# Five more slots for expert weights in the mixers' memory, and a new order of the experts' widths

## The chip, the cores and the metric

The kernel runs on one core of a Trainium2 chip. The metric is the device time of one execution in microseconds (us). The engines of the core are TensorE (PE, with PEld for its weight loads), VectorE (DVE), ScalarE (ACT), GpSimd (POOL) and SyncE (SP); DMA queues feed the core's memory.

## What is computed

The reference is a two-layer encoder trunk on x of 1 x 256 x 1024, in float32. Each layer runs four token mixers, merges them through gates, projects the sum, normalises it, and then runs a channel mixer: dense on layer 0, two of eight experts for each token on layer 1. The change concerns the experts:

```python
def moe_swiglu(x, router, w1, w3, w2):
    bsz, seq, d = x.shape
    t = x.reshape(bsz * seq, d)
    logits = (t @ router).astype(jnp.float32)
    top_val, top_idx = lax.top_k(logits, TOP_K)
    probs = jax.nn.softmax(top_val, axis=-1)
    combine = jnp.sum(jax.nn.one_hot(top_idx, N_EXPERTS, dtype=jnp.float32) * probs[..., None], axis=1)
    out = jnp.zeros((bsz * seq, d), jnp.float32)
    for e in range(N_EXPERTS):
        out = out + combine[:, e:e + 1] * swiglu(t, w1[e], w3[e], w2[e])
    return out.astype(x.dtype).reshape(bsz, seq, d)
```

An expert is 1024 x 3584 (w1 and w3) and 3584 x 1024 (w2).

## The kernel before

Layer by layer the mixers, the gated merge, the output projection and the channel mixer follow each other. All large weights stream from HBM in units through a ring of four slots (`ring`, 1536 KB each); SP issues the loads in a fixed order and waits before each for the unit that held the slot.

**Experts.** One expert's weights are 28 units of 1536 KB, each with 128 of the 3584 inner columns: the two up matrices and the down matrix. Eight experts make 224 units. For them the ring has seven slots, the four of `ring` and three more in the mixers' scratch (`extra`, in `arena`), named `ex_slot`. Units go to the slots in turn, and a slot is reloaded when the down product of its unit is done (`unit_used`).

Seven units form a block, four blocks an expert. TensorE runs, for each unit, `hidden` (the two up products, L1161: 32 products in 64-column strips) and `down` (16 products, L1081); ACT and DVE form the activation between them (L1460, L2241). Once a block follow a gather of the next expert's tokens (L1151) and the product that adds a part of the previous expert's result to the sum (L1108), just before the block's last `down`. At the start of an expert the weights of its tokens are turned (L1062).

**Places.** The experts run in eight places, each with a fixed width in token columns, `PLACES`: 80 five times, then 88, 72, 72. Expert 0 always has place 0, so that its weights can be loaded before the router has chosen. The others are ranked by their number of tokens, and `TURN` gives the rank for each place. If an expert has more tokens than its place has columns, a further pass over all experts runs; the program reads the number of passes from memory.

**Code.** The width is fixed in the instructions, so places of one width share code. `CLASSES` gives the runs of places, (0, 5), (5, 6), (6, 8): for each run TensorE's program has one body of a block, in a loop over the four blocks inside a loop over the run's places. ACT and DVE have code for each place.

**Before the experts** SP issues the loads of the output projection, then the first three expert units into `extra` (wait `ml_done`), then four into the ring as the projection frees its units (L2352), and then waits for `unit_used` (L2357) at each unit. `mg_done` counts the merges that DVE ends with L1977. `proj`, `brT`, `gate_more`, `s5_tab`, `pm` and most of `cst` are tables and buffers of the mixers; the experts read none of them but some constants.

## Time and profile before

| what | value |
|---|---|
| median of 3 runs | 1773.6 us (1773.14 to 1776.63) |
| the profiled execution | 1776.6 us |
| its span, first to last instruction | 1774.8 us |
| PE busy, PEld busy | 1705.5 us (96%), 1516.6 us (85%) |
| DVE busy, ACT busy | 850.4 us (48%), 369.8 us (21%) |
| moved by DMA | 473.52 MB, mean 267 GB/s |
| granted TensorE clock, mean | 0.992 |

The span is what the rows below are measured in; 1.8 us of the profiled execution lie outside it. A busy PE is not PE at its peak, since products are pipelined and their ends modelled. Slice by slice the DMA is nearly full only in the second half of the span, which is the experts. A window row gives the busy us of each engine in a stretch and in brackets the instructions that ran there. A timeline row merges neighbouring instructions of one line; in brackets stands the idle time before it and what ended it, where "issue" is a wait for nothing that the profile shows. A queue row gives packets, MB and the share of 16 DMA engines' time.

### The profile page before, as it was taken

How to read it: one execution, taken by the hardware profiler on the slowest of the kernel's cores; microseconds unless marked ns; L12 is line 12 of the kernel's file. 1: busy time of each engine (PE TensorE's matmuls, PEld its weight loads, DVE VectorE, ACT ScalarE, POOL GpSimd, SP SyncE). 2: the span in 40 equal slices, each digit the busy share in tenths (PEclk: the TensorE clock that was granted, in tenths of full speed). 3: DMA queues.
4: the chain of work that ended last, by engine and by line, in shares of the span. 5: the costliest groups of instructions: out<-in, count | busy, mean ns of one | idle time of the engine just before them, and what ended most of it. 6: DMA issues, size and time to landing. Idle time of an engine off the chain costs nothing.

```text
span 1774.8 us, 66051 instructions
## 1 busy us (share of the span) xinstructions
PE 1705.5 (96%) x29752; PEld 1516.6 (85%) x29752; DVE 850.4 (48%) x2075; ACT 369.8 (21%) x876; POOL 2.9 (0%) x12
## 2 busy tenths in 40 slices
PE   7999999999998999999999999999999999999997
PEld 6878888599945888887769999999999999999886
DVE  6986755367777696766342232222223222232224
ACT  5443422101102635343120000000000000001001
POOL 0000000000000000000000000000000000000000
PEclk9999999999999999999989999999999999999999
DMA  8332223444444323322549999999999999999994
GB/s 319 111 116 101 101 90 120 153 146 171 173 160 170 142 96 107 107 97 73 199 193 375 426 426 426 426 426 425 427 426 426 426 424 385 405 395 426 425 426 203
DMA packets 56708, 473.52 MB, mean 267 GB/s; under 512 B 5456, under 2 KB 5744, under 8 KB 21136
## 3 DMA queue, kind: packets, MB, share of 16 engines
q1 hardware_dynamic: 55040, 463.49, 65.1%
q10 hardware_dynamic: 1184, 5.82, 0.9%
q0 software_dynamic: 368, 2.64, 0.4%
q8 instruction: 76, 1.25, 0.3%
q14 instruction: 40, 0.33, 0.1%
HBM read 470.86 MB, written 1.06 MB: 266 GB/s over the span
## 4 chain that ended last, share of the span: by engine, by line
PE 76%; DMA 16%; DVE 5%; issue 2%; ACT 1%; SPq 0%; DVEq 0%; ACTq 0%
PE bank L1161 18%; DMA ring<-in_moe 16%; PE bank L900 11%; PE bank L1081 10%; PE bank L554 9%; PE bank L961 7%; PE bank L917 3%; PE bank L939 3%; PE bank L996 3%; PE bank L1108 2%; PE bank L1151 1%; PE bank L533 1%; PE bank L680 1%; PE bank L728 1%; PE bank L811 1%
## 5 line engine op out<-in xcount | busy, mean ns | idle before, releaser
L1161 PE MATMUL bank<-arena,ring 128*64 128x80 f32 (+2 forms) x8192 | 307.5, 233 | 17.6 <-DMA ring<-in_moe 12.5
L1161 PEld LDWEIGHTS bank<-arena,ring 128*64 128x64 f32 x8192 | 291.5, 138 | 25.7 <-DMA ring<-in_moe 12.8
L2241 DVE TENSOR_TENSOR arena<-arena,bank 128x80 f32<-128x80 f32 (+2 forms) x224 | 52.8, 236 | 516.7 <-ACT arena L1460 516.7
L900 PE MATMUL bank<-xT,ring 128*128 128x256 f32 x1024 | 227.8, 381 | 4.8 <-DVE arena L1778 4.8
L1161 PE MATMUL bank<-arena 128*64 128x80 f32 (+2 forms) x6144 | 223.2, 232 | 2.8 <-DMA arena<-in_moe 1.4
L900 PEld LDWEIGHTS bank<-xT,ring 128*128 128x128 f32 x1024 | 192.8, 190 | 34.6 <-issue 8.9
L1161 PEld LDWEIGHTS bank<-arena 128*64 128x64 f32 x6144 | 214.8, 137 | 6.3 <-issue 2.5
L1460 ACT ACTIVATE arena<-bank 128x80 f32<-128x80 f32 (+3 forms) x226 | 53.6, 238 | 713.6 <-PE bank L1161 705.7
L1081 PE MATMUL bank<-arena,ring 128*64 128x80 f32 (+2 forms) x4096 | 163.7, 232 | 3.4 <-issue 3.4
L554 PE MATMUL bank<-xT,ring 128*128 128x256 f32 x704 | 156.3, 383 | 8.1 <-DMA ring<-in_w_in 8.1
L1081 PEld LDWEIGHTS bank<-arena,ring 128*64 128x64 f32 x4096 | 153.8, 137 | 7.9 <-issue 3.9
L554 PEld LDWEIGHTS bank<-xT,ring 128*128 128x128 f32 x704 | 134.2, 192 | 29.4 <-DMA ring<-in_w_in 8.1
L1081 PE MATMUL bank<-arena 128*64 128x80 f32 (+2 forms) x3072 | 122.1, 232 | 3.1 <-issue 2.3
L1081 PEld LDWEIGHTS bank<-arena 128*64 128x64 f32 x3072 | 112.7, 137 | 3.4 <-issue 2.5
L2248 DVE STREAM_TRANSPOSE arena<-arena 32x64 f32<-32x64 f32 x384 | 90.1, 235 | 6.5
L917 PE MATMUL bank<-brT,ring 128*128 128x256 f32 x256 | 61.9, 387 | 0.0
L961 PE MATMUL bank<-arena 128*128 128x128 f32 x480 | 56.9, 275 | 0.0
L939 PE MATMUL bank<-ring,x_tok 128*128 128x512 f32 x128 | 55.3, 592 | 0.0
L961 PEld LDWEIGHTS bank<-arena 128*128 128x128 f32 x480 | 55.2, 192 | 0.0
L917 PEld LDWEIGHTS bank<-brT,ring 128*128 128x128 f32 x256 | 46.9, 190 | 7.8 <-issue 1.0
L939 PEld LDWEIGHTS bank<-ring,x_tok 128*128 128x128 f32 x128 | 24.3, 190 | 29.8 <-issue 29.7
L996 PE MATMUL bank<-arena 128*128 128x512 f32 x88 | 41.6, 594 | 0.3 <-DVE arena L2078 0.3
(454 smaller groups left out, 1802.8 us busy)
## 6 DMA issues: line engine op xcount, KB each, us to landing
ring<-in_moe SPq DMA_DIRECT2D x128, 1536.0 KB, 17.7
arena<-in_moe SPq DMA_DIRECT2D x96, 1536.0 KB, 16.4
ring<-in_w_gate SPq DMA_DIRECT2D x32, 1024.0 KB, 4.9
ring<-in_ffn_up SPq DMA_DIRECT2D x22, 1024.0 KB, 4.8
ring<-in_w_in SPq DMA_DIRECT2D x14, 1536.0 KB, 7.0
ring<-in_ffn_down SPq DMA_DIRECT2D x11, 1024.0 KB, 4.8
ring<-in_w_branch SPq DMA_DIRECT2D x8, 1024.0 KB, 5.0
ring<-in_w_out SPq DMA_DIRECT2D x8, 1024.0 KB, 6.3
```

What stands on the lines that cost most here:

```text
L554: last = mm(b[:, (j % 2) * T:(j % 2 + 1) * T], w[:, i, kt * P:(kt + 1) * P], xT[:, kt, :], start=(kt == 0), stop=(kt == KT - 1))
L900: last = mm(two(b)[:, q, :], w[:, q, kt * P:(kt + 1) * P], xT[:, kt, :], start=(kt == 0), stop=(kt == KT - 1))
L917: last = mm(two(b)[:, q, :], w[:, ct, (2 * k + q) * P:(2 * k + q + 1) * P], brT[:, br, ct, :], start=(ct == 0), stop=(ct == 1))
L939: last = mm(b[k][:, :], merged[:, kt, (k // 2) * P:(k // 2 + 1) * P], w[:, c, (k % 2) * 512:(k % 2 + 1) * 512], start=False, stop=(kt == K ...
L961: last = mm(out, left[:, k * P:(k + 1) * P], right[:, k, :], start=(k == 0), stop=(k == 3))
L996: last = mm(banks[DOWN_BANK[name]][:, :], left, right, start=(p == 0 and name in ("P1", "P6", "P7")), stop=end, skip_group_check=True)
L1081: last = mm(banks[2 + dt // 4][c:c + STRIP, dt % 4 * CAP:dt % 4 * CAP + n], ex_slot[s][:, o:o + STRIP], ACTIVE_H[:, s, 0:n], start=(s == 0 ...
L1108: last = mm(banks[5][c:c + STRIP, tt * 2 * P:(tt + 1) * 2 * P], selwT[0:CAP, tt * P + c:tt * P + c + STRIP], ys_part[0:CAP, :], start=True ...
L1161: last = mm(bank[c:c + STRIP, g * CAP:g * CAP + n], w[:, at:at + STRIP], rhs[:, kt, 0:n], start=(kt == 0), stop=(kt == KT - 1), skip_group ...
L1460: f(ff_sl[:, i % 2, 0:n], bank[:, 0:n], ACT.Silu).then_inc(S["h_silu"], 1)
L2241: tt_(ACTIVE_H[:, i, 0:PLACES[e]], ff_sl[:, s % 2, 0:PLACES[e]], bank[:, CAP:CAP + PLACES[e]], ALU.mult)\
L2248: ins = nc.vector.transpose(ys_part[32 * j:32 * j + 32, :].rearrange("p (n d) -> p n d", n=2)[:, :, 32 * i:32 * i + 32], yT[32 * i:32 * i ...
```

## The change

Five more slots, `late_slot`, lie over the mixers' buffers, which are put into one tile `home` in an order that leaves free of them what the experts still read. The router's weights move to a tile of their own, and the constants are reordered and loaded in three parts, not two.

The five slots hold units 0 to 4 of place 0; SP loads them once all merges are done (`mg_done` at 8). The seven slots of the ring start with unit 5. As soon as place 0 has used a late slot, SP loads into it a unit of place 6 (`LATE_AT`), the first five of that place. From unit 12 on the ring goes on as before, except that place 6 takes its first five units from the late slots.

The widths become 80, 80, 72, 72, 88, 72, 72, 72, with the ranks 0, 2, 3, 4, 1, 5, 6, 7. Which slots a block uses is fixed in its code, so `CLASSES` gets seven runs, and the first blocks of places 0 and 6 have a body of their own ahead of the loop over the other three.

```diff
-PLACES = (80,) * 5 + (88, 72, 72)
-CLASSES = ((0, 5), (5, 6), (6, 8))
-TURN = (0, 2, 3, 4, 5, 1, 7, 6)
+PLACES = (80,) * 2 + (72,) * 2 + (88,) + (72,) * 3
+CLASSES = ((0, 1), (1, 2), (2, 4), (4, 5), (5, 6), (6, 7), (7, 8))
+TURN = (0, 2, 3, 4, 1, 5, 6, 7)
+LATE = 5
+LATE_AT = 6
...
-EARLY = CO["ident"][0]
+EARLY = (CO["trow"][0], CO["ident"][0])
+MIXER_CONSTANTS = CO["eps"][0]
...
+        sizes = [NTILE * PITCH, NBR * 2 * T, 2 * 512, 24 * 16, NPM, NCO]
+        ends = list(itertools.accumulate(sizes))
+        home = sb("home", [P, ends[-1]])
+        assert LATE * UNIT <= ends[-2] + MIXER_CONSTANTS
+        proj, brT, gate_more, s5_tab, pm, cst = (home[:, e - n:e] for e, n in zip(ends, sizes))
+        proj = proj.rearrange("p (a b) -> p a b", a=NTILE)
+        brT = brT.rearrange("p (a b t) -> p a b t", a=NBR, b=2)
+        s5_tab = s5_tab.rearrange("p (a b) -> p a b", a=24)
+        late_slot = [home[:, UNIT * k:UNIT * (k + 1)] for k in range(LATE)]
...
+        LATE_BLOCK = LATE_AT * BLOCKS
+        ring_loads = [(NE * EX_STEPS - 2 * LATE - q + EX_RING - 1) // EX_RING for q in range(EX_RING)]
+
+        def unit_home(k, i):
+
+            if k in (0, LATE_BLOCK) and i < LATE:
+                return None, 1 + (k > 0)
+            at = EX_RING * k + i - LATE * (1 + (k >= LATE_BLOCK and (k, i) >= (LATE_BLOCK, LATE)))
+            return at % EX_RING, at // EX_RING + 1
+
+        def freed_by(k, i):
+
+            if k in (0, LATE_BLOCK) and i < LATE:
+                return i
+            n = EX_RING * k + i
+            ahead = [m for m in range(n) if unit_home(m // EX_RING, m % EX_RING)[0] == unit_home(k, i)[0]]
+            return ahead[-1]
...
-                def block(it, at, n):
-                    loads = pe.snap(at * 16)
+                def block(ps, it, at, k, k0, n):
+
                     steps = pe.snap(at * EX_RING)
+                    home_of = [unit_home(k0, i) for i in range(EX_RING)]
+                    tiles = [late_slot[i] if q is None else ex_slot[q] for i, (q, _) in enumerate(home_of)]
+                    in_pass = {n: pe.snap((ps * n + (k - k0 + 1)) * 16) for n in sorted(set(ring_loads))}
+                    late = pe.snap(ps * 32 + 16) if k0 in (0, LATE_BLOCK) else None
 
                     def hidden(s):
-                        sem_, before = ex_loaded[s]
-                        pe.wait_ge(sem_, loads + 16 * (before + 1))
+                        q, number = home_of[s]
+                        if q is None:
+                            pe.wait_ge(late_loaded[s], late + 16 * (number - 1))
+                        else:
+                            sem_, before = ex_loaded[q]
+                            pe.wait_ge(sem_, in_pass[ring_loads[q]] + 16 * (before + number - 1))
 
                         pe.wait_ge(S["h_ready"], steps + (h0 + s - HIDDEN_LAST[s] + 1))
-                        strips(ex_slot[s], xg, banks[HIDDEN_BANK[s]], n)
+                        strips(tiles[s], xg, banks[HIDDEN_BANK[s]], n)
...
-                            with pe.Fori(0, BLOCKS) as b:
-                                block(it, pe.snap(it * BLOCKS + b), PLACES[first])
+                            start = first * BLOCKS in (0, LATE_BLOCK)
+                            if start:
+                                block(ps, it, pe.snap(it * BLOCKS), first * BLOCKS, first * BLOCKS, PLACES[first])
+                            with pe.Fori(int(start), BLOCKS) as b:
+                                block(ps, it, pe.snap(it * BLOCKS + b), e * BLOCKS + b, first * BLOCKS + start,
+                                      PLACES[first])
...
-                        act.dma_start(cst[:, EARLY:NCO], A["cst"][:, EARLY:NCO]).then_inc(S["cst_loaded"], 16)
+                        for o in (slice(0, EARLY[0]), slice(EARLY[1], NCO)):
+                            act.dma_start(cst[:, o], A["cst"][:, o]).then_inc(S["cst_loaded"], 16)
...
-            for s in range(EX_RING):
-                if s >= len(extra):
-                    name, value = unit_end[first_ff[1] + s - len(extra) - RING]
-                    sp.wait_ge(S[name], value)
-                sp.dma_start(ex_slot[s], A["moe"][0, s]).then_inc(ex_loaded[s][0], 16)
-
-            def expert_unit(steps, s, src):
-
-                sp.wait_ge(S["unit_used"], steps + (used_before["experts"] + s - EX_RING + 1))
-                sp.dma_start(ex_slot[s % EX_RING], src).then_inc(ex_loaded[s % EX_RING][0], 16)
+            def first_unit(q):
+                return A["moe"][0, LATE + q]
+
+            for q in range(len(extra)):
+                sp.dma_start(ex_slot[q], first_unit(q)).then_inc(ex_loaded[q][0], 16)
...
+            sp.wait_ge(S["mg_done"], 4 * DEPTH)
+            for i in range(LATE):
+                sp.dma_start(late_slot[i], A["moe"][0, i]).then_inc(late_loaded[i], 16)
+            for q in range(len(extra), EX_RING):
+                name, value = unit_end[first_ff[1] + q - len(extra) - RING]
+                sp.wait_ge(S[name], value)
+                sp.dma_start(ex_slot[q], first_unit(q)).then_inc(ex_loaded[q][0], 16)
...
+            used = used_before["experts"]
+
+            def one_pass(ps, loaded):
+
+                done = ps * (NE * EX_STEPS)
+                late_unit = sp.value_load(ex_id[0:1, LATE_AT:LATE_AT + 1], min_val=0, max_val=NE - 1) * EX_STEPS
+                for i in range(LATE):
+                    sp.wait_ge(S["unit_used"], done + (used + i + 1))
+                    row = sp.snap(late_unit + i)
+                    sp.dma_start(late_slot[i], all_units[bass.ds(row, 1)].rearrange("o p c -> p (o c)"))\
+                        .then_inc(late_loaded[i], 16)
+                for s in range(loaded, EX_STEPS):
+                    k, i = s // EX_RING, s % EX_RING
+                    q = unit_home(k, i)[0]
+                    sp.wait_ge(S["unit_used"], done + (used + freed_by(k, i) + 1))
+                    sp.dma_start(ex_slot[q], A["moe"][0, s]).then_inc(ex_loaded[q][0], 16)
                 for e in range(1, NE):
                     unit = sp.value_load(ex_id[0:1, e:e + 1], min_val=0, max_val=NE - 1) * EX_STEPS
-                    with sp.Fori(0, BLOCKS) as b:
+
+                    def load_block(b, k0, first=0):
                         steps = sp.snap((ps * NE + e) * EX_STEPS + b * EX_RING)
-                        for i in range(EX_RING):
-                            sp.wait_ge(S["unit_used"], steps + (used_before["experts"] + i - EX_RING + 1))
+                        for i in range(first, EX_RING):
+                            q = unit_home(k0, i)[0]
+                            sp.wait_ge(S["unit_used"], steps + (used + freed_by(k0, i) - EX_RING * k0 + 1))
                             row = sp.snap(unit + b * EX_RING + i)
-                            sp.dma_start(ex_slot[i], all_units[bass.ds(row, 1)].rearrange("o p c -> p (o c)"))\
-                                .then_inc(ex_loaded[i][0], 16)
+                            sp.dma_start(ex_slot[q], all_units[bass.ds(row, 1)].rearrange("o p c -> p (o c)"))\
+                                .then_inc(ex_loaded[q][0], 16)
+
+                    if e == LATE_AT:
+                        for b in range(2):
+                            load_block(b, e * BLOCKS + b, 0 if b else LATE)
+                        with sp.Fori(2, BLOCKS) as b:
+                            load_block(b, e * BLOCKS + 2)
+                    else:
+                        with sp.Fori(0, BLOCKS) as b:
+                            load_block(b, e * BLOCKS)
...
+            pool.dma_start(router_w[:, :], A["router"]).then_inc(S["router_loaded"], 16)
```

SP's queue from the last weights of the output projection to the second round of expert units, before (`home` is the tile that the late slots lie in; `arena` holds the three extra slots):

```order
L2336 DMA ring<-in_w_out 128x2048 [waits bank_filled] x4
L2352 DMA arena<-in_moe 128x3072 [waits ml_done]
L2352 DMA arena<-in_moe 128x3072 x2
L2352 DMA ring<-in_moe 128x3072 [waits unit_used] x3
L2352 DMA ring<-in_moe 128x3072 [waits bank_filled]
L2357 DMA arena<-in_moe 128x3072 [waits unit_used,ids_ready,passes_ready]
L2357 DMA arena<-in_moe 128x3072 [waits unit_used] x2
L2357 DMA ring<-in_moe 128x3072 [waits unit_used] x4
```

and now:

```order
L2377 DMA ring<-in_w_out 128x2048 [waits bank_filled] x4
L2393 DMA arena<-in_moe 128x3072 [waits ml_done]
L2393 DMA arena<-in_moe 128x3072 x2
L2396 DMA home<-in_moe 128x3072 [waits mg_done]
L2396 DMA home<-in_moe 128x3072 x4
L2400 DMA ring<-in_moe 128x3072 [waits unit_used] x3
L2400 DMA ring<-in_moe 128x3072 [waits bank_filled]
L2408 TENSOR_LOAD ex_id [waits ids_ready,passes_ready]
L2408 ISA x2
L2412 ISA [waits unit_used]
L2412 DMA home<-in_moe 128x3072
L2412 ISA [waits unit_used]
```

Five loads into `home` stand between the three extra units and the four ring units, and behind these a read of place 6's expert and five loads that each wait for a used unit.

PE's program at the end of the first body and the start of the next, before (L1108 is the once-a-block product, L1062 the turn at the start of an expert, L1125 and L1122 the loops over blocks and places):

```order
L1151 MATMUL bank<-arena 64x88 x8
L1108 MATMUL bank<-arena 64x256 x4
L1077 REGISTER_ALU
L1081 MATMUL bank<-arena,ring 64x80 x16
L1125 REGISTER_ALU
L1125 COMPARE_AND_BRANCH
L1122 REGISTER_ALU
L1122 COMPARE_AND_BRANCH
L1122 UNCONDITIONAL_BRANCH
L1115 ISA
L1062 MATMUL bank<-cst,arena 64x128 x4
L1125 UNCONDITIONAL_BRANCH
```

and now at the end of place 0's first block, which no loop repeats (L1144 is the old L1108, L1164 the loop over blocks):

```order
L1191 MATMUL bank<-arena 64x88 x8
L1144 MATMUL bank<-arena 64x256 x4
L1113 REGISTER_ALU
L1117 MATMUL bank<-arena 64x80 x16
L1164 UNCONDITIONAL_BRANCH
L1107 ISA
L1109 ISA
L1201 MATMUL bank<-arena 64x80 x32
```

and at the end of the next body, that of place 0's other three blocks (L1158 is the loop over places, L1090 the old L1062):

```order
L1144 MATMUL bank<-arena 64x256 x4
L1113 REGISTER_ALU
L1117 MATMUL bank<-arena 64x80 x16
L1164 REGISTER_ALU
L1164 COMPARE_AND_BRANCH
L1158 REGISTER_ALU
L1158 COMPARE_AND_BRANCH
L1158 UNCONDITIONAL_BRANCH
L1151 ISA
L1090 MATMUL bank<-home,arena 64x128 x4
L1164 UNCONDITIONAL_BRANCH
```

Before, the second body is reached after twenty blocks; now the second is reached after one block and the third, again 80 wide, after four. L1108 stood three times in PE's program; L1144 stands nine times.

## Rows read from the trace of the kernel before

**Rows 1.** The page: GB/s moved in 40 equal slices of the span.

```profile
GB/s 319 111 116 101 101 90 120 153 146 171 173 160 170 142 96 107 107 97 73 199 193 375 426 426 426 426 426 425 427 426 426 426 424 385 405 395 426 425 426 203
```

**Rows 2.** Windows of places 1 and 4: busy us by engine, clock, DMA, GB/s.

```profile
1027.00:1127.00 100.00, 99.97 (x2800) 98.50 (x2798) 28.16 (x102) 9.11 (x32) 0.00 (x0) 1.00 1.01 426
1335.00:1439.00 104.00, 102.30 (x2790) 98.83 (x2787) 28.18 (x102) 9.12 (x32) 0.00 (x0) 1.00 1.01 426
```

**Rows 3.** PE timeline, one L1108 group a block: start, us, line, shapes, count.

```profile
952.80 1.10 PE L1108 MATMUL bank<-arena 88*64 88x256 f32 x8
...
1027.26 1.04 PE L1108 MATMUL bank<-arena 88*64 88x256 f32 x8
...
1127.19 1.04 PE L1108 MATMUL bank<-arena 88*64 88x256 f32 x8
...
1230.89 1.04 PE L1108 MATMUL bank<-arena 88*64 88x256 f32 x8
...
1439.52 1.04 PE L1108 MATMUL bank<-arena 88*64 88x256 f32 x8
...
1526.79 1.04 PE L1108 MATMUL bank<-arena 88*64 88x256 f32 x8
...
1553.79 1.04 PE L1108 MATMUL bank<-arena 88*64 88x256 f32 x8
...
1582.54 1.09 PE L1108 MATMUL bank<-arena 88*64 88x256 f32 x8
...
1627.95 1.04 PE L1108 MATMUL bank<-arena 88*64 88x256 f32 x8
...
1755.84 1.04 PE L1108 MATMUL bank<-arena 88*64 88x256 f32 x8
```

**Rows 4.** DMA queues of 956:1440, then q8 in 1440:1475 and 1555:1587.

```profile
q1 hardware_dynamic: 18822, 205.59, 100.7%
q14 instruction: 11, 0.09, 0.0%
...
q8 instruction: 5, 0.08, 0.9%
...
q8 instruction: 5, 0.08, 1.0%
```

**Rows 5.** PE timeline, pieces that began after a stall; [idle before <-releaser].

```profile
939.59 1.60 PE L1161 MATMUL bank<-arena,ring 128*64 128x80 f32 x40 [0.40 <-issue]
...
945.60 0.56 PE L1161 MATMUL bank<-arena,ring 128*64 128x80 f32 x9 [1.36 <-issue]
...
951.79 0.56 PE L1081 MATMUL bank<-arena,ring 128*64 128x80 f32 x10 [1.62 <-issue]
...
1461.22 1.05 PE L1081 MATMUL bank<-arena,ring 128*64 128x88 f32 x22 [1.15 <-issue]
...
1570.98 0.35 PE L1081 MATMUL bank<-arena 128*64 128x72 f32 x5 [2.33 <-issue]
```

**Rows 6.** Timelines of SP, DVE and PE before the experts; window 910:931.

```profile
877.89 1.63 SPq L2352 DMA_DIRECT2D arena<-in_moe  x3
884.39 20.93 SPq L2352 DMA_DIRECT2D ring<-in_moe  x4
931.83 6.90 SPq L2357 DMA_DIRECT2D arena<-in_moe  x3
...
878.30 0.69 DVE L1977 TENSOR_TENSOR x_tok<-x_tok,arena 128x512 f32<-128x512 f32 x1
...
924.54 0.66 PE L1062 MATMUL bank<-cst,arena 128*64 128x128 f32 x8 [0.16 <-issue]
...
910.00:931.00 21.00, 20.10 (x314) 19.30 (x316) 13.09 (x68) 7.79 (x13) 0.00 (x0) 0.69 0.03 10
```

**Rows 7.** Window 795:818 (columns as in 2) and its queue q8.

```profile
795.00:818.00 23.00, 21.82 (x594) 18.09 (x590) 12.97 (x28) 3.99 (x10) 0.00 (x0) 1.00 0.19 60
...
q8 instruction: 5, 0.08, 1.5%
```

More of the change, by code:

```diff
@@ L78 @@
 CO = {}
-for _name, _n in [("trow", T), ("eps", 8), ("ones", P), ("ident", P), ("mean64", P), ("sum64", P), ("rot", P), ("cos", T), ("sin", T), ("cmask", 4 * CH),
-                  ("lmask", 12 * CH), ("reset", T), ("win", 2 * 3 * P), ("before", P),
-                  ("cap", CAP), ("eye64", CH), ("e8", NE), ("tie", NE), ("places", 3 * NE), ("skip", NE), ("turn", NE),
+for _name, _n in [("mean64", P), ("sum64", P), ("rot", P), ("cos", T), ("sin", T), ("cmask", 4 * CH),
+                  ("lmask", 12 * CH), ("reset", T), ("win", 2 * 3 * P), ("eye64", CH), ("trow", T),
+                  ("eps", 8), ("ones", P), ("ident", P), ("before", P), ("cap", CAP), ("e8", NE), ("tie", NE), ("places", 3 * NE), ("skip", NE), ("turn", NE),
                   ("resid", 3 * P)]:
@@ L228, in encoder @@
         slot_loaded = [sem(f"slot{i}_loaded") for i in range(RING)]
+        late_loaded = [sem(f"late{i}_loaded") for i in range(LATE)]
         extra_loaded = [sem(f"extra{i}_loaded") for i in range(EX_RING - RING)]
@@ L522, in route_first @@
                         last = mm(banks[6][c:c + STRIP, tt * NE:(tt + 1) * NE], xT[:, kt, o:o + STRIP],
-                                  M("router", kt * NE, NE), start=(tt == kt == 0), stop=(kt == KT - 1),
+                                  router_w[:, kt * NE:(kt + 1) * NE], start=(tt == kt == 0), stop=(kt == KT - 1),
                                   skip_group_check=True)
@@ L2380, in _ @@
                 with sp.Fori(1, passes) as ps:
-                    for s in range(EX_RING):
-                        expert_unit(ps * (NE * EX_STEPS), s, A["moe"][0, s])
-                    one_pass(ps)
+                    sp.wait_ge(S["unit_used"], ps * (NE * EX_STEPS) + used)
+                    for i in range(LATE):
+                        sp.dma_start(late_slot[i], A["moe"][0, i]).then_inc(late_loaded[i], 16)
+                    for q in range(EX_RING):
+                        sp.dma_start(ex_slot[q], first_unit(q)).then_inc(ex_loaded[q][0], 16)
+                    one_pass(ps, LATE + EX_RING)
             for n in range(2 * TT):
```

28 lines of the change are left out of this document (11 added, 17 removed).

## The prediction

> **What bounds the kernel now.** The page's slices come first: from about 960 us to the end of the experts the transfers run at 426 GB/s, with a dip to 385 and 405 [rows 1]. All of it is expert weights, units of 1536 KB, so one unit takes 1.573 MB / 426 GB/s = 3.69 us and a block of seven 25.8 us. The windows by place show who waits for whom: at 1027 to 1127 us (place 1, 80 columns) TensorE is busy for 99.97 of 100 us, at 1335 to 1439 us (place 4, also 80) the transfers are as full but one place takes 104 us [rows 2]. So TensorE runs off the lead that the seven slots held, and then goes at the DMA's pace.
>
> The PE timeline gives both paces. L1108 runs once a block, so from one L1108 to a later one is a whole number of blocks [rows 3]. TensorE's own pace at 80 columns: 952.80 to 1027.26 is three blocks, 24.8 us each; one place is 99.93 us (to 1127.19), so a change of expert adds 0.7. At 88 columns: 1526.79 to 1553.79, 27.0. At 72: 1582.54 to 1627.95 is two blocks, 22.7. The DMA's pace: 1230.89 to 1439.52 is two places at 104.3, or 26.1 a block. The lead of a full ring: 952.80 to 1230.89 took 278.1 us for 11 blocks that cost the DMA 287; the slots were worth 8.8 us.
>
> The third bound is TensorE's code. A loop body for one block is a new stretch of code the first time that it runs. While bodies repeat (956 to 1440 us) the queue q8 moves nothing; in 1440 to 1475 (first block of place 5) and 1555 to 1587 (first of place 6) it moves 5 packets each, 0.08 MB [rows 4]. In these stretches TensorE sits idle on "issue", with no wait for data: 1.15 us for one packet in place 5, 2.33 for one in place 6; in the very first body 0.40, 1.36 and 1.62 [rows 5]. By whole blocks: place 5 takes 114.27 us (1439.52 to 1553.79) where 4 x 27.0 + 0.7 = 108.7, so its body costs 5.5; place 6's first block takes 28.75 (to 1582.54) where 22.7 + 0.7 + 0.2 (the old place's last, wider product) = 23.6, so 5.1; the first body's three stalls sum to 3.4.
>
> **The change, part by part.** *Five early units.* SP issues the three extra units at 877.89, ring units from 884.39 on as the output projection frees slots, and then nothing until 931.83; from 910 to 931 the DMA moves 10 GB/s [rows 6]. The new queue puts five loads between the extra units and the ring. Their wait, mg_done, ends with the last merge on DVE, 878.30 + 0.69 = 879.0, about when the third extra unit is issued, so it costs nothing. Twelve units at 3.69 from about 880 end near 925, when the experts start (the turn of the first expert's weights stands at 924.54). 5 x 3.7 = 18.5 us of transfers leave the loaded stretch. The ring units land up to 18 us later than before, but they are now units 8 to 11, not needed before about 950. Cost: nothing; the router's small work now runs beside full transfers, 0 to 1.5 us.
>
> *The refill for place 6.* The five freed slots reload at once with place 6's first units, before unit 12. So up to place 5 the loads stand exactly as before (12 + n - 5 = 7 + n units after n loads) and the 18.5 us come back in place 6, whose first block needs two ring units, 7.5 us of DMA, not 26.1.
>
> *Places.* TensorE's own work becomes 2 of 80, 5 of 72, one of 88 columns: 3 places go from 80 to 72, 3 x 4 x (24.8 - 22.7) = 25 us less. By the reference's router on its inputs, the experts hold 48, 71, 60, 61, 62, 70, 55 and 85 tokens; expert 0 goes to place 0, the others by rank fit (71 in 80, 70 and 62 in 72, 85 in 88, the rest in 72), so one pass as before.
>
> *Bodies.* PE's program had three stretches with L1108 (now L1144), one a body; the new one has nine: eight after the first, where there were two, each 3.4 to 5.5 by the three samples. Above: the 2.33 stall at 72 columns, four times, is 9. I take 5.2, near the two samples that, like the new bodies, run beside full transfers; the 3.4 had an empty DMA queue at first.
>
> *The rest* (a split constants load, one more ACT issue; router weights loaded by POOL at the start; a few register operations a block) lies beside TensorE's first 60 us or in its queue: 0, at most 1 us.
>
> **The sum** is a ledger by block. A block takes TensorE's own time (plus 0.7 at a change of expert, plus 5.2 for a new body). The lead grows by that less 26.1, is capped at 8.8, and what falls below zero is waited. On the kernel before it gives 1756.5 for the last L1108, where the trace has 1755.84. The new order, from 952.80 with a full lead: place 0, 3 x 24.8 + 5.2 = 79.6 (lead 6.2 at its end). Place 1, 105.1 (4.9). Place 2, 96.7 + 2.8 waited = 99.5 (0). Place 3, all DMA, 104.4. Place 4, 27.7 + 5.2 + 81 = 113.9 (8.8). Place 5, 98.1, of it 1.4 waited. Place 6, two new bodies, 91.5 + 10.4 = 101.9, no wait (2.0). Place 7, 96.7 + 5.7 = 102.4. The last L1108 is at 1757.7, or 1.2 us later than the ledger's before. The 18.5 us of transfers and the 25 us of columns are real, but six bodies at 5.2 eat them. What follows the experts is unchanged. The profiled execution took 1776.6 us against the median of 1773.6; I carry the difference over to the median: 1773.6 + 1.2 = 1774.8. With 4.5 to 5.8 a body the ledger gives -3.0 to +4.8, so 1771 to 1778 for this case.
>
> **A rule weighed.** Where the DMA is nearly idle, 795 to 818 us, five code packets go by and TensorE is busy for 21.82 of 23 us; in the expert stage each packet cost about 1 us [rows 5, 7]. The Trainium skill ("Runtime: NRT & Kernel Launch", Instruction fetch mechanics) says that a sequencer fetches the next 16 KiB page while it runs the current one, so that crossing a page is mostly hidden; the stretch at 795 agrees, the expert stage does not. By that rule the six bodies would be free, which is the end of the first rival.
>
> **Rivals.** *Code loads are cheap* (up to 4.5 us a body). Where the slots are full the DMA goes idle, and a packet may then come faster; place 6's new bodies stand there. At 3.4 a body the ledger gives -9.2, 1764; at 0 it gives -14.9, 1759, and there TensorE waits for the DMA again in places 2, 3, 5, 6 and 7. For it: the 3.4 sample and the idle stretch. Against: both loaded samples. Chance 0.34, of it 0.05 for free ones.
>
> *Code loads are dear* (over 5.8). A narrower block runs through its code faster, so each packet shows more: 2.33 us against 1.15 [rows 5]; five of the eight later bodies are 72 wide. At 7.0 a body the ledger gives +12.4, 1786. It decides from 5.6 a body, where +3.5 is passed. Against: place 6 before was 72 wide too and cost 5.1. Chance 0.27.
>
> *The change doesn't do what it says*: the early loads start late (every unit that does not land before 931 costs up to 3.7 us again) or a second pass starts. The merge's end at 879.0 and the token counts speak against both. Some 10 us slower; chance 0.03.
>
> **How the numbers follow.** My forecast, bodies at 4.5 to 5.8, has 0.36. About 0.2%, 3.5 us, is what a measurement of this kernel can tell from no change. The cheap case is faster (0.34), the forecast lies nearly within 0.2% (0.36), the dear and the failing case are slower (0.30). The range reaches from 3.4 to just under 7 a body: 1764 to 1785.
>
> **What would show it.** Right: twelve expert issues before the experts start, DMA full from 880 to about 925; five q8 packets at each of the first blocks of places 0 (second block too), 1, 2, 4, 5, 6 (twice), 7, and idle on issue there; place 2 near 99, 3 near 104, 4 near 114, 6 near 102. Cheap loads: first blocks at 26 to 27 us and waits for DMA in place 7 of over 7 us. Dear: place 7 with hardly a wait for DMA and first blocks over 30 us at 72 columns. It would be wrong in kind if TensorE waited for units in place 0 or 6, or if a block that repeats were slower than 24.8, 27.0 and 22.7.

## The result and the profile after

The changed kernel takes 1786.8 us (median of five runs, 1785.41 to 1791.97) against 1773.93 for the kernel before in the same comparison: 12.9 us more, a ratio of 1.0070 with a 95% interval of 1.0054 to 1.0087. That is slower by more than the 0.2% that can be told from no change, and 1.8 us past the top of the predicted range. The profiled execution took 1787.19 us with a span of 1785.4. The profiled execution before, 1776.6 us, was the slowest of its five, so the two traces below differ by 10.6 us where the medians differ by 12.9.

The page of the changed kernel, against [rows 1]: GB/s by slices, the queue of code packets (q8), and the chain of work that ended last, by engine. The last two stand in the page of the kernel before as well, shown behind.

```profile
GB/s 316 112 116 105 102 80 119 152 149 173 174 162 159 142 97 115 114 77 73 220 377 360 396 399 416 425 406 426 426 425 424 425 408 391 426 305 380 424 417 206
...
q8 instruction: 109, 1.79, 0.4%
...
PE 84%; DVE 5%; DMA 5%; issue 4%; ACT 1%; DVEq 0%; SPq 0%; ACTq 0%
```

```profile
q8 instruction: 76, 1.25, 0.3%
...
PE 76%; DMA 16%; DVE 5%; issue 2%; ACT 1%; SPq 0%; DVEq 0%; ACTq 0%
```

The twenty-first slice has 377 now, where [rows 1] has 193: the early units are loaded there. But the row no longer stands at 425 in the expert stage; it dips again and again, because the slots are full and TensorE is late. In the chain of work DMA goes from 16% to 5% and issue from 2% to 4%: TensorE waits less for data and more for its own instructions. The 33 code packets more, for six more bodies, are 5.5 packets of 16 KB a body.

The early part came as the prediction said. SP's timeline (start, length, line, count), and windows of the changed kernel (us; PE, PEld, DVE, ACT and POOL busy; granted clock; DMA share; GB/s):

```profile
880.86 1.59 SPq L2393 DMA_DIRECT2D arena<-in_moe  x3
882.50 2.46 SPq L2396 DMA_DIRECT2D home<-in_moe  x5
887.35 20.93 SPq L2400 DMA_DIRECT2D ring<-in_moe  x4
932.29 16.34 SPq L2412 DMA_DIRECT2D home<-in_moe  x5
...
880.00:925.00 45.00, 42.51 (x309) 25.74 (x309) 17.87 (x64) 9.03 (x22) 0.00 (x0) 0.96 0.98 410
```

Twelve units are asked for before the experts start, and the DMA moves 410 GB/s from 880 to 925. The five freed slots are refilled from 932 on. Where the time went shows in the block ends, as in [rows 3] (L1144 is the old L1108). Rows of TensorE's timeline, each the L1144 group at the end of a block: of place 0's first and last block, then of the first and the last block of places 1 and 2, the last of place 3, the first and the last of places 4 and 5, the first, second and last of place 6, the first and last of place 7.

```profile
953.00 0.38 PE L1144 MATMUL bank<-arena 88*64 88x256 f32 x1
...
1035.47 1.04 PE L1144 MATMUL bank<-arena 88*64 88x256 f32 x8
1067.88 0.38 PE L1144 MATMUL bank<-arena 88*64 88x256 f32 x1
...
1142.65 1.04 PE L1144 MATMUL bank<-arena 88*64 88x256 f32 x8
1173.60 1.33 PE L1144 MATMUL bank<-arena 88*64 88x256 f32 x7
...
1242.25 1.04 PE L1144 MATMUL bank<-arena 88*64 88x256 f32 x8
...
1345.02 1.04 PE L1144 MATMUL bank<-arena 88*64 88x256 f32 x8
1377.35 1.03 PE L1144 MATMUL bank<-arena 88*64 88x256 f32 x8
1458.58 1.04 PE L1144 MATMUL bank<-arena 88*64 88x256 f32 x8
1490.11 1.04 PE L1144 MATMUL bank<-arena 88*64 88x256 f32 x8
1558.37 1.04 PE L1144 MATMUL bank<-arena 88*64 88x256 f32 x8
1587.38 0.38 PE L1144 MATMUL bank<-arena 88*64 88x256 f32 x1
1619.22 1.43 PE L1144 MATMUL bank<-arena 88*64 88x256 f32 x8
1664.98 1.04 PE L1144 MATMUL bank<-arena 88*64 88x256 f32 x8
1697.03 0.38 PE L1144 MATMUL bank<-arena 88*64 88x256 f32 x1
...
1766.43 1.04 PE L1144 MATMUL bank<-arena 88*64 88x256 f32 x8
```

The first expert block ends at 953.00 (952.80 before) and the last L1144 stands at 1766.43 (1755.84 before). These 10.6 us are the whole difference between the two spans, so it arises in these eight places:

| place | columns | predicted us | measured us | TensorE's own work | excess over that |
|---|---|---|---|---|---|
| 0 (three blocks) | 80 | 79.6 | 82.5 | 74.4 | 8.1, one body |
| 1 | 80 | 105.1 | 107.2 | 99.9 | 7.3, one body |
| 2 | 72 | 99.5 | 99.6 | 91.5 | 8.1, one body |
| 3 | 72 | 104.4 | 102.8 | 91.5 | 11.3, waits for data |
| 4 | 88 | 113.9 | 113.6 | 108.7 | 4.9, one body |
| 5 | 72 | 98.1 | 99.8 | 91.5 | 8.3, one body |
| 6 | 72 | 101.9 | 106.6 | 91.5 | 15.1, two bodies |
| 7 | 72 | 102.4 | 101.4 | 91.5 | 9.9, one body |

A place is the distance of two of these rows; its own work is four blocks at 24.8, 27.0 or 22.7 plus 0.7, as in the prediction. Outside place 3 TensorE's waits (953 to 1766.5) have none for data, so the excess is the bodies': 61.7 us for eight, 7.7 each, where the prediction took 5.2. Of the 61.7 us TensorE is idle on issue for 48.2; in the rest it counts as busy, some of it at a lower clock (below).

Read by blocks it is simpler than that. Place 0's second block, the first of the eight, lasts 31.3 us, and the new blocks of the places above last 32.4 (1035.47 to 1067.88), 30.9, 32.3, 31.5, 29.0, 31.8 and 32.1 us. Only 29.0 stands out, and the columns don't matter: 80, then 80, 72, 88, 72, 72, 72, 72. In place 7's first block the stalls come in an even beat. TensorE's timeline, pieces that began after a stall:

```profile
1673.97 0.41 PE L1117 MATMUL bank<-arena,ring 128*64 128x72 f32 x6 [1.39 <-issue]
...
1680.02 1.47 PE L1201 MATMUL bank<-arena 128*64 128x72 f32 x40 [1.85 <-issue]
...
1686.53 0.53 PE L1201 MATMUL bank<-arena 128*64 128x72 f32 x9 [2.29 <-issue]
...
1693.11 0.53 PE L1117 MATMUL bank<-arena 128*64 128x72 f32 x10 [2.43 <-issue]
```

Stalls end 6.05, 6.51 and 6.58 us apart, and the five packets of code that this block gets, at some 6.3 us, are 31.5 us. So I read it as this: the block takes as long as its code takes to come, not its own work plus a charge. The idle time on issue fits. It is 4.0 us in place 4's first block (88 columns), 6.1 in place 1's (80), 6.6 and 7.9 in those of places 2 and 7 (72), each time in four stalls: the less a block has to compute, the more of the same wait shows. What the DMA did in such blocks, in windows of the changed kernel (place 0's second block, the first of places 1 and 4, both new blocks of place 6, the first of place 7), and of the kernel before (its two later bodies, places 5 and 6; place 5's block ends at 1471.78, after 32.3 us, so its window is 1 us too long):

```profile
953.00:984.30 31.30, 27.29 (x703) 26.76 (x700) 6.63 (x24) 2.28 (x8) 0.00 (x0) 0.95 0.91 350
1035.50:1067.90 32.40, 26.27 (x709) 25.24 (x707) 8.31 (x30) 2.28 (x8) 0.00 (x0) 1.00 0.98 405
...
1345.00:1377.30 32.30, 28.32 (x710) 27.25 (x708) 8.31 (x30) 2.32 (x8) 0.00 (x0) 1.00 1.01 424
...
1558.40:1587.40 29.00, 23.60 (x708) 22.92 (x706) 8.20 (x30) 2.23 (x8) 0.00 (x0) 1.00 0.69 291
1587.40:1619.20 31.80, 24.67 (x701) 24.19 (x699) 6.50 (x24) 2.23 (x8) 0.00 (x0) 0.96 0.91 346
1665.00:1697.00 32.00, 24.03 (x708) 23.03 (x704) 8.20 (x30) 2.23 (x8) 0.00 (x0) 1.00 1.01 422
```

```profile
1439.50:1472.80 33.30, 29.33 (x723) 28.26 (x721) 9.02 (x32) 2.94 (x9) 0.00 (x0) 1.00 1.01 420
1553.80:1582.50 28.70, 25.43 (x709) 24.78 (x705) 8.33 (x30) 2.23 (x8) 0.00 (x0) 0.94 0.96 378
```

The one short first block of the changed kernel (29.0) is the one with the least traffic (0.69), and of the two samples before, the shorter had the emptier queue (378 against 420 GB/s). The share of a whole block doesn't settle it, though: place 0's second block and place 6's second had 0.91 and took 31.3 and 31.8 us all the same. That gave the theory: **a code packet waits behind expert weights on its DMA engine, the next one is asked for only late, and a first block under full transfers takes 31 to 32 us whatever its width.** The rivals: TensorE's code comes at this rate anyway; or the slots, the refill or the new widths do harm of their own.

### The profile page after: what moved, and what is told of

The parts are those of the page before. It is cut to its first block, busy times and chain, and to the rows that moved or that the text cites. A ratio compares the mean times of both kernels' runs of the same rounds, so it can differ in the third digit from the quotient of the medians.

```text
span 1785.4 us, 66083 instructions
## 1 busy us (share of the span) xinstructions
PE 1680.0 (94%) x29752; PEld 1491.8 (84%) x29752; DVE 849.0 (48%) x2075; ACT 369.4 (21%) x876; POOL 3.4 (0%) x13
## 4 chain that ended last, share of the span: by engine, by line
PE 84%; DVE 5%; DMA 5%; issue 4%; ACT 1%; DVEq 0%; SPq 0%; ACTq 0%
PE bank L1201 24%; PE bank L1117 12%; PE bank L928 11%; PE bank L582 9%; PE bank L989 7%; DMA arena<-in_moe 4%; PE bank L945 3%; PE bank L967 3%; PE bank L1024 3%; PE bank L1144 2%; PE bank L1191 1%; PE bank L708 1%; PE bank L756 1%; PE bank L561 1%; PE bank L839 1%
## 5 line engine op out<-in xcount | busy, mean ns | idle before, releaser
L2282 DVE TENSOR_TENSOR arena<-arena,bank 128x72 f32<-128x72 f32 (+2 forms) x224 | 52.1, 233 | 518.2 <-ACT arena L1501 517.1
L1201 PE MATMUL bank<-arena,ring 128*64 128x72 f32 (+2 forms) x7744 | 279.0, 230 | 14.7 <-issue 11.3
L1201 PEld LDWEIGHTS bank<-arena,ring 128*64 128x64 f32 x7744 | 266.4, 137 | 18.0 <-issue 13.1
L1201 PE MATMUL bank<-arena 128*64 128x72 f32 (+2 forms) x5952 | 218.0, 230 | 20.5 <-issue 16.0
L1201 PEld LDWEIGHTS bank<-arena 128*64 128x64 f32 x5952 | 206.2, 137 | 25.9 <-issue 22.6
L1501 ACT ACTIVATE arena<-bank 128x72 f32<-128x72 f32 (+3 forms) x226 | 53.1, 235 | 721.5 <-PE bank L1201 713.5
L1117 PE MATMUL bank<-arena,ring 128*64 128x72 f32 (+2 forms) x3872 | 153.7, 231 | 7.9 <-issue 7.9
L1117 PEld LDWEIGHTS bank<-arena,ring 128*64 128x64 f32 x3872 | 142.3, 138 | 9.7 <-issue 8.9
L1117 PE MATMUL bank<-arena 128*64 128x72 f32 (+2 forms) x2976 | 118.3, 230 | 9.6 <-issue 9.4
L1117 PEld LDWEIGHTS bank<-arena 128*64 128x64 f32 x2976 | 110.8, 138 | 13.4 <-issue 10.6
L945 PE MATMUL bank<-home,ring 128*128 128x256 f32 x256 | 61.9, 387 | 0.0
L945 PEld LDWEIGHTS bank<-home,ring 128*128 128x128 f32 x256 | 46.9, 190 | 7.8 <-issue 1.0
L1264 ACT ACTIVATE home<-bank,small 128x256 f32<-128x256 f32 x48 | 20.1, 469 | 112.1 <-PE bank L928 106.8
## 6 DMA issues: line engine op xcount, KB each, us to landing
ring<-in_moe SPq DMA_DIRECT2D x121, 1536.0 KB, 10.6
```

The source lines that it names most:

```text
L945: last = mm(two(b)[:, q, :], w[:, ct, (2 * k + q) * P:(2 * k + q + 1) * P], brT[:, br, ct, :], start=(ct == 0), stop=(ct == 1))
L1117: last = mm(banks[2 + dt // 4][c:c + STRIP, dt % 4 * CAP:dt % 4 * CAP + n], tiles[s][:, o:o + STRIP], ACTIVE_H[:, s, 0:n], start=(s == 0 a ...
L1201: last = mm(bank[c:c + STRIP, g * CAP:g * CAP + n], w[:, at:at + STRIP], rhs[:, kt, 0:n], start=(kt == 0), stop=(kt == KT - 1), skip_group ...
L1501: f(ff_sl[:, i % 2, 0:n], bank[:, 0:n], ACT.Silu).then_inc(S["h_silu"], 1)
L2282: tt_(ACTIVE_H[:, i, 0:PLACES[e]], ff_sl[:, s % 2, 0:PLACES[e]], bank[:, CAP:CAP + PLACES[e]], ALU.mult)\
```

## The experiments

**Take the traffic away.** Every reload moves one eighth of its columns (in short; `PARTW` in the kernel):

```diff
-sp.dma_start(ex_slot[q], all_units[...])
+sp.dma_start(ex_slot[q][:, 0:UNIT // 8], all_units[...][:, 0:UNIT // 8])
```

> The changed kernel, but every reload of an expert unit (all but the first 12 units) moves one eighth of its columns; seven eighths of the reloaded expert weights are left out, so the experts' result is not the reference's, and the DMA engines are nearly idle while the experts run. Instructions, bodies, widths and waits stay. Theory (code packets wait behind expert weights on the DMA engines; with full transfers a body's first block takes 31 to 32.4 us at any width): first blocks fall towards TensorE's own pace, 24 to 27 us at 80 and 72 columns and 28 to 29 at 88, all other blocks at 24.8, 27.0 and 22.7 with no wait for data; the last L1144 comes at 1690 to 1710 us, run 1712 to 1730. Rival (the code loads at a rate of its own, whatever the DMA does): first blocks stay at 31 to 32 us, the last L1144 near 1745, run near 1766. In both cases the transfers' own limit (places 2 and 3) is gone, so only the first blocks' length tells them apart.

1710.63 us in one execution, 1.4 below the expected range. A window over the repeating experts, and the block ends around the first blocks of places 2 and 7 (L1145 is L1144 here):

```profile
1024.00:1690.00 666.00, 665.34 (x19546) 654.09 (x19544) 195.21 (x714) 62.95 (x224) 0.00 (x0) 1.00 0.20 56
```

```profile
1123.82 1.04 PE L1145 MATMUL bank<-arena 88*64 88x256 f32 x8
1147.08 1.04 PE L1145 MATMUL bank<-arena 88*64 88x256 f32 x8
...
1598.12 1.04 PE L1145 MATMUL bank<-arena 88*64 88x256 f32 x8
1621.70 0.38 PE L1145 MATMUL bank<-arena 88*64 88x256 f32 x1
```

The same code packets (109 on q8 here too) now cost next to nothing: 23.3 and 23.6 us for first blocks whose own work is 23.4, and TensorE is busy for 665.34 of 666 us. The rival "the code's own rate" falls. The Trainium skill ("Runtime: NRT & Kernel Launch", Instruction fetch mechanics) says that a page is fetched while the current one runs and that crossing is mostly hidden. This run agrees with it at a DMA share of 0.20; the changed kernel, at 0.97 over the same stretch, doesn't.

**How it grows with the traffic.** The same with half and with three quarters of the columns.

> The changed kernel with reloads of half the columns; the other half of the reloaded expert weights is left out, so the experts' result is not the reference's. The rows are 6 KB as in the run with two transfers a unit, but the DMA engines are busy about half the time. It measures how the cost of a body grows with the load. Theory (the next code packet is asked for only when TensorE has entered the last one, and waits in the engine's queue behind whatever expert data are there: 1.3 us from the end of a stall to the next packet with no data, 3.8 with full transfers, plus 2.4 us until TensorE goes on): about 5 us a packet, first blocks of 72 columns at 23 to 26 us, of 80 columns at 25 to 27. Rival (any traffic from the expert queue is enough): 30 us and more.

> The same with reloads of three quarters of the columns; a quarter of the reloaded weights is left out. The DMA engines are busy some 75 to 85% of the time. Theory: between the half and the whole, 5.5 us a packet, first blocks of 72 columns at 26 to 29 us, of 80 at 27 to 30. Rival (the wait appears only when the engines are never free): as with half the columns.

1724.28 and 1737.74 us, one execution each. Windows over the repeating experts, half first:

```profile
1027.00:1703.00 676.00, 667.31 (x19540) 655.06 (x19538) 195.31 (x714) 63.01 (x224) 0.00 (x0) 1.00 0.69 218
```

```profile
1030.00:1717.00 687.00, 670.03 (x19568) 657.63 (x19566) 195.31 (x714) 62.99 (x224) 0.00 (x0) 1.00 0.86 322
```

The mean of the eight later first blocks is 24.2 us at a DMA share of 0.20, 25.6 at 0.69, 27.0 at 0.86 and 31.4 at 0.97 (the changed kernel). Both expectations held within 1 us (the engines were busier than I had put it: 0.69, not half). By the trace's records of single packets, a code packet of the changed kernel starts 3.3 to 4.3 us after the last one where the DMA engines are idle, and 5.2 to 7.2, in the mean 6.3, where they are full; in the runs with half and three quarters both kinds stand side by side, with some between. That the share sets how often a packet meets data is read from this, not shown. At 72 columns a block uses up a packet's code in about 4.1 us (22.7 us for 5.5 packets), so a packet every 6.3 us leaves TensorE idle for some 2.2; at 88 columns (27.0 us, 4.9 a packet) for 1.4. That is why the widest place lost least.

**The bodies alone.** The kernel before, its old widths, in seven runs:

```diff
-CLASSES = ((0, 5), (5, 6), (6, 8))
+CLASSES = ((0, 1), (1, 2), (2, 4), (4, 5), (5, 6), (6, 7), (7, 8))
```

> The kernel before with one edit: its eight places are coded as seven runs instead of three, at the old widths (80 five times, 88, 72, 72), so TensorE gets four more bodies (places 1, 2, 4, 7) and nothing else changes. Theory (a first block takes 31 to 32.4 us whatever its width): the new bodies add 7 us each at 80 columns and 8 to 9 at 72, of which the waits for data that they replace in places 2, 4 and 7 give some back; the ledger with first blocks of 32 us gives +10 us, with 7 to 7.6 a body +11 to +14. My prediction's 5.2 a body gives +2. Rival (bodies cost little and the slots or the refill made the changed kernel slow): 0, within 2 us of the kernel before.

1783.37 us, ratio 1.0042 (1.0028 to 1.0056): 8.2 slower than the kernel before in the same comparison, with not one byte of weights or column changed. New first blocks of places 1 (80 columns) and 7 (72):

```profile
1025.87 1.04 PE L1108 MATMUL bank<-arena 88*64 88x256 f32 x8
1057.74 1.09 PE L1108 MATMUL bank<-arena 88*64 88x256 f32 x8
...
1659.54 1.04 PE L1108 MATMUL bank<-arena 88*64 88x256 f32 x8
1690.93 1.04 PE L1108 MATMUL bank<-arena 88*64 88x256 f32 x8
```

They take 31.9 and 31.4 us where their own work is 25.5 and 23.4: one duration, two costs. The other new bodies, at places 2 and 4 (80 columns), take 31.6 and 34.0; the two that were there before, 30.8 at 88 columns and 31.6 at 72. So it is 31 to 34 us rather than 31 to 32 (the granted clock was 0.95 in the block of 34.0). This is the cleanest of the runs; the ledger's +10 was 2 too high.

**The widths alone**, on the kernel before:

```diff
-PLACES = (80,) * 5 + (88, 72, 72)
-CLASSES = ((0, 5), (5, 6), (6, 8))
-TURN = (0, 2, 3, 4, 5, 1, 7, 6)
+PLACES = (80,) * 2 + (72,) * 2 + (88,) + (72,) * 3
+CLASSES = ((0, 2), (2, 4), (4, 5), (5, 8))
+TURN = (0, 2, 3, 4, 1, 5, 6, 7)
```

> The kernel before with the new widths alone (80, 80, 72, 72, 88, 72, 72, 72, the turn of the places with them), coded as four runs, so one body more than before; no new slots. Theory: the 25 us of columns saved turn into waits for data, since the places of 72 columns run at the DMA's 26.1 us a block; the ledger gives -0.2 at 5.2 a body and +3 at 7. Rival (the narrower places pay by themselves): 8 us or more faster. Rival (the new order of widths harms): more than 6 us slower.

1773.36 us, ratio 0.9991 (0.9981 to 1.0001): no difference that can be told. The 25 us of columns turn into waits for data, as the ledger had it at 5.2 a body; its +3 at 7 a body lies outside the interval. TensorE's waits (line, releaser: us in all, times, longest) in places 6 and 7 of this run, where 15.3 us are for data of the ring (9.4 more stand at the end of place 2 and in place 3):

```profile
PE bank L1161 <- DMA ring<-in_moe: 15.3, 32, 0.6
```

**The slots alone**: the changed kernel at the old widths and turn, `CLASSES = ((0, 1), (1, 5), (5, 6), (6, 7), (7, 8))`.

> The kernel with the five slots alone: the changed kernel at the old widths and turn (80 five times, 88, 72, 72), coded as five runs (place 0, places 1 to 4, 5, 6, 7), refill for place 6 as in the change; six bodies beyond the first (place 0's second block, places 1, 5, 6 twice, 7). Theory (each first block 31 to 32 us): the slots' 18.5 us are eaten by the bodies, the ledger with first blocks of 32 us gives 16 us more than the kernel before; since it gives the changed kernel 16 too and measured 13, 8 to 16 slower here. My prediction's 5.2 a body gives about +2. Rival (the harm comes from the new widths): within 3 us of the kernel before, or faster.

1783.96 us, ratio 1.0054 (1.0036 to 1.0072), 8.0 slower than the kernel before: at the lower edge of the theory's 8 to 16 (the ledger itself gave 16), and far from the rival. Against the prediction's price this time proves nothing: the expectation's "about +2" at 5.2 a body is a slip, since the ledger, gone through by places (79.6, 105.1, 99.9, 104.0, 104.4, 113.9, 101.9, 102.4), gives between +7 and +8. Its first blocks take 30.4 (place 0's second), 31.5, 32.2, 24.5 and 29.2 (place 6's two) and 30.7. The short one is again place 6's first, whose units are in their slots already. So even without the new widths the slots are worth less than the bodies that come with them.

**Fewer bodies, all else as in the change.** Places 0 and 1 share their repeated block, and places 6 and 7; the turn of an expert's weights moves to the end of the expert before it, in the same order:

```diff
-CLASSES = ((0, 1), (1, 2), (2, 4), (4, 5), (5, 6), (6, 7), (7, 8))
+CLASSES = ((0, 2), (2, 4), (4, 5), (5, 6), (6, 8))
...
-with pe.Fori(int(start), BLOCKS) as b:
+lo = pe.snap((e + 1) % 2) if start and end - first == 2 else int(start)
+with pe.Fori(lo, BLOCKS) as b:
```

> The changed kernel with fewer bodies and nothing else: places 0 and 1 share one body for their repeated blocks (an inner loop that starts at block 1 for the first expert and at block 0 for the second), and so do places 6 and 7; the turns keep their order. Slots, refill, widths and transfers are those of the change; the first blocks of places 1 and 7 no longer run new code, so six bodies beyond the first instead of eight. Theory: these two first blocks fall from 32.4 and 32.1 us to 25 and 23 to 26, place 7 waits for data again (about 9 us in all, as the ledger with the measured 31 us a first block and 25.9 a block of transfers has it), and the run is 4 to 8 us faster than the changed kernel: 1779 to 1783. Rival (slots, refill or order of widths cost the time): no change, 1786 to 1788.

1782.84 us, ratio 1.0048 (1.0031 to 1.0065) to the kernel before, where the change has 1.0070: about 4 us back by the ratios, 6 by the medians, as expected (1782.84 lies just inside 1779 to 1783, and the two intervals overlap a little). The first blocks of places 1 and 7, with their old code:

```profile
1033.01 1.04 PE L1144 MATMUL bank<-arena 88*64 88x256 f32 x8
1058.46 1.04 PE L1144 MATMUL bank<-arena 88*64 88x256 f32 x8
...
1661.95 1.04 PE L1144 MATMUL bank<-arena 88*64 88x256 f32 x8
1685.27 1.04 PE L1144 MATMUL bank<-arena 88*64 88x256 f32 x8
...
1760.58 1.04 PE L1144 MATMUL bank<-arena 88*64 88x256 f32 x8
```

25.5 and 23.3 us, their own pace. Of these 15.7 us less than in the change, some goes to waits for data in place 7 (2 us in each of its last two blocks), and places 2 to 6 were 0.5 to 2 us longer each; the last L1144 comes 5.9 us earlier. The granted clock is one visible part of that: 0.90 in the first block of place 5 and 0.94 in both new blocks of place 6, against 0.95, 1.00 and 0.96 in the change. The ledger with first blocks of 31.4 us and 25.9 us of transfers a block gives 1760 for the last L1144, where 1760.58 was measured. By the same ledger no choice of widths and of the refilled place gets the slots below the kernel before; that was only reckoned, not run.

**Shorten the wait by smaller transfers.** Three forms, all on the changed kernel. If a code packet waits for the transfer at the head of its engine, smaller pieces should let it in sooner. First, four transfers of 32 partitions a unit (in short):

```diff
-sp.dma_start(ex_slot[q], src).then_inc(sem, 16)
+for c in range(4):
+    r = slice(c * P // 4, (c + 1) * P // 4)
+    sp.dma_start(ex_slot[q][r, :], src[r, :]).then_inc(sem, 16)
```

> The changed kernel with each expert unit loaded by four transfers of 32 partitions instead of one of 128, same bytes and same order. Theory in its narrow form (a code packet waits until the transfer at the head of a DMA engine is through, so shorter transfers shorten the wait): first blocks fall from 31 to 32.4 us to 26 to 29, and the run to 1760 to 1778 us. If the wait is set by the share of the engines' time and not by the length of one transfer, or by the code alone: first blocks at 31 to 32 us and 1785 to 1789 us. If four issues a unit load SP's queue: waits for data in places that had none, and above 1790 us.

2266.59 us, ratio 1.2803. The expectation's worst case, above 1790 us, was meant for another reason, a loaded SP queue. A window of it:

```profile
1100.00:1200.00 100.00, 63.62 (x1400) 60.60 (x1400) 14.94 (x54) 4.56 (x16) 0.00 (x0) 0.88 1.01 226
```

The engines are busy all the time (1.01) and move 226 GB/s instead of 426: a 12 KB packet takes 0.86 us instead of 0.46. The rate is not the same throughout: from 1450 to 1600 us the same transfers move 378 GB/s, again at a share of 1.01. The run says nothing on the idea, but code packets, too, come 9 to 10 us apart in the slow stretch. Beside the run with half the columns that tells something else. There the DMA moved 218 GB/s, hardly less, at a share of 0.69, and the first blocks took 25.6 us in the mean. So the bytes moved in a second are not what holds the code up; full engines fit both runs. Then the cut through the columns, in two and in three, which keeps all 128 partitions in each transfer:

> The changed kernel with each expert unit loaded as two transfers of half the columns, so that rows (and packets) are 6 KB instead of 12 KB and all 128 partitions take part. Theory in its second form: a code packet waits for a fixed number of about eight packets ahead of it on its DMA engine. It comes from two runs: from the end of a stall to the next code packet 3.8 to 4.0 us pass where a 12 KB packet takes 0.460 us (8.4 packets), and about 7.4 us where the same 12 KB, written to 32 partitions, take 0.861 us (8.6 packets). With 6 KB packets at about 0.235 us the wait is 1.9 us, the interval of code packets falls from 6.2 to 4.3, and first blocks from 31 to 32 us to 24 to 26. Smaller packets cost the transfers about 2% (0.469 us for 12 KB), so blocks that wait for data go from 25.9 to 26.5; the run comes to 1770 to 1778. Rival (the wait is set by the engines' share of busy time, whatever the packets are): first blocks stay at 31 to 32 and the run ends at 1787 to 1796.

> The same with three transfers of a third of the columns (4 KB rows, about 0.16 us a packet). Eight packets are 1.3 us, an interval of 3.7 us, below what a block at 72 columns needs (22.7 us for five packets is 4.5): first blocks at TensorE's own pace plus under 1 us, but transfers 3 to 4% slower, blocks that wait for data near 27, run 1776 to 1788. Rival (share of busy time): first blocks at 31 to 32 and a run above 1790.

1795.44 us (ratio 1.0121, 1.0099 to 1.0142) and 1803.34 us (one execution): where the rivals had them, 1787 to 1796 and above 1790. Stalls in place 7's first block, two pieces and then three:

```profile
1676.38 0.41 PE L1125 MATMUL bank<-arena,ring 128*64 128x72 f32 x6 [1.06 <-issue]
...
1682.70 1.73 PE L1209 MATMUL bank<-arena 128*64 128x72 f32 x40 [2.13 <-issue]
```

```profile
1685.35 0.41 PE L1125 MATMUL bank<-arena,ring 128*64 128x72 f32 x6 [1.12 <-issue]
...
1691.67 1.47 PE L1209 MATMUL bank<-arena 128*64 128x72 f32 x40 [2.12 <-issue]
```

Two stalls end 6.32 us apart in both, with rows of 12, 6 or 4 KB, so the second form of my theory (about eight packets ahead) is wrong. The wait does not follow the size of a packet or of a transfer, as the rival (the engines' share of busy time) said. Only the cost of smaller packets was right: blocks that wait for data went from 25.8 to 26.4 and 26.9 us. The Trainium skill ("DMA: Bandwidth & Descriptors", Queues, rings and completion order) says that an engine takes its queues in turn, a whole packet of one before it goes to the next (by that page a packet is some 9 to 17 descriptors, not the single row that the profile counts). These traces don't record which engine a code packet used or what stood ahead of it, so the order itself isn't shown; no shortening with the transfer shows in these runs.

## Why the prediction was wrong

**The failed step is "Bodies ... I take 5.2".** The mechanism was named (a new body's code comes in five packets and TensorE idles on issue), its count was right (eight later bodies, 109 packets where there were 76), and its place in the sum too. Its size was not: 7.7 on average. Three things were wrong in how it was sized.

- I read a cost to be added from two samples. What stays nearly the same is the duration of the first block. Place 5 before is 88 columns wide, with 27.7 us of own work under a first block of 32.3: the least that any body here shows under full transfers. A block of 72 columns pays 8 to 9 under the same transfers.
- I used place 6 before (5.1 at 72 columns) as the witness that narrow blocks pay no more. It ran just behind the wide place, with the slots full: 378 GB/s in its first block, and 4.3 us between two of its code packets. It was the exception, and that stood in the same trace; that the emptier queue was the reason is likely, but no run tests it, and two blocks of the changed kernel with a share of 0.91 paid the full price.
- That 5.1 wasn't all code, either. TensorE was idle on issue for 3.3 us in the block (0.94 and 2.33), and from 1571.6 to 1575.0 the granted clock was 0.50, which costs half of these 3.4 us. The window's 0.94 shows it, and the prediction took it for the price of a body.

**The dear rival was the right one**, by its mechanism ("a narrower block runs through its code faster, so each packet shows more") and nearly by its price: 7.0 a body and 1786, measured 7.7 and 1786.8. Its signs came too: place 7 had no wait for DMA, and its first block took 32.1 us at 72 columns. It had 0.27. That 1786 stood so near is in part luck: at 7.7 the same ledger overshoots (below). Its evidence, 2.33 us of stall against 1.15 [rows 5], was the better reading, and I let the block sum of place 6 outweigh it.

**The cheap rival** reckoned that packets come faster where the DMA goes idle. That is true (29.0 us in place 6's first new block, and the runs with lighter reloads), but the DMA was idle in few of the new bodies: its share was 0.91 or more in seven of eight.

**What held.** Early units, refill and DMA from 880 to 925 came as written. TensorE didn't wait for units in place 0 or 6, and repeating blocks kept 24.8 to 25.0, 27.1 and 22.7, except that the block behind a new one was up to 1.7 us longer (26.5 in place 0). Place 3 took 102.8 (104.4 forecast), place 2 99.6 (99.5), place 4 113.6 (113.9); in place 4 the body cost 4.9, since it is the 88-wide one. That the widths alone bring nothing was the ledger's -0.2 and is measured as -0.1%. With 7.7 for each body the ledger goes to +17 where 10.6 came, mostly because it then charges 7.7 also at 88 columns (2.8 too much) and holds 26.1 us of transfers a block, where place 3 has 25.7 (1.6 in all).

**Where the gain went.** The 18.5 us of early transfers and the 25 us of columns only help while the DMA is the limit. A first block of 31.4 us is 5.6 longer than the transfers of its seven units (25.8), and a full ring is worth 8.8 us of lead. So after one or two new bodies the slots are full and the transfers pause: the dips in the GB/s row. Six more bodies than before, at 7.7 us in the mean, and a ring that can't store the pause: that is the loss.

**A smaller part is the clock.** In place 6's second block the granted clock is 0.96, in place 0's second and place 5's first 0.95, against 1.00 in the others. In each of the three TensorE ran at the lower of its two levels (1.2 GHz) for some 3.4 us (0.50 at 964.6, 1483.4 and 1616.5), just after a stall of over 2 us. That is 1.7 us lost each time, 5.1 in all, where the kernel before lost 1.7 in its experts. The first blocks at 1.00 last as long (32.4, 32.3, 32.1 us), so little of it seems to add to the time; how much is open. That full DMA engines make the new code late is shown by the runs with lighter reloads. Where the packet waits, and what fixes the beat of 6.2 to 6.3 us, was not found: it is longer where the transfers are slower (9 to 10 us at 226 GB/s) and doesn't depend on the packet's size, which would fit a fixed amount of data ahead of a code packet, but no run tested that.

## What to carry over

Count the program's bodies before splitting a loop by width or by buffer: while transfers fill the DMA engines, the first pass through some 90 KB of new code took 31 to 34 us here however little there was to compute, and the narrower the block, the more of it is loss. A price taken from a sample should be asked whether it is a sum or a maximum; here two widths side by side (as in the run with the bodies alone) would have told. And savings on the limiting transfers count only if buffers can hold what arrives during the stalls that the saving brings with it.

## What was not expected of the hardware

- Five code packets, 0.08 MB beside some 13 MB of weights in the same 32 us, set TensorE's pace: 6.2 to 6.3 us from one to the next under full expert transfers, 3.3 to 4.3 with the engines idle.
- The same units moved as four transfers of 32 partitions went at 226 GB/s (1100 to 1200 us) and 378 (1450 to 1600) instead of 426, with the engines as busy (share 1.01 each time). Cut by columns into 6 or 4 KB rows it lost only 2 and 4%.
